# Hybrid decoder layer, one core: four units of the dilated projection as seven products, with the seventh product's bank copied out by VectorE

## The chip, the cores and the metric

The kernel runs on one core of a Trainium2 chip. The metric is the device time of one execution in microseconds, the median of several runs. A core has five engines that run their own instruction streams in order and wait for each other through semaphores: TensorE (PE) for matmuls, VectorE (DVE), ScalarE (ACT), GpSimd (POOL) and SyncE (SP), which here only issues transfers. Sixteen DMA engines move the data of all queues.

## The reference

One decoder layer on x of 256 x 2048 in float32:

```
h = rms_norm(x, g_attn); proj = h @ w_in          # 2048 x 10248
o_a = fox_attention(...)        # 8 heads of 128
o_b = dilated_attention(...)    # 8 heads of 128
merged = sigmoid(ga) * (o_a @ w_br_fox) + sigmoid(gb) * (o_b @ w_br_dil)   # each 1024 x 2048
x = x + merged @ w_out
h = rms_norm(x, g_ffn)
x = x + conv_ffn(h)             # 2048 -> 2 x 5632, causal convolution, SwiGLU, -> 2048
```

The change is in `o_b @ w_br_dil`: 256 rows, K = 1024 (eight heads of 128), 2048 columns.

## The kernel before

**Units.** The weights come in tiles of two K blocks by 512 columns (128 x 1024 numbers, 512 KB). A tile is a unit, and units have one running number. SP loads the tile (into one of four slots of `raw`, or into `raw_x` and `raw_y` for sums), ScalarE writes its high part into one of six slots of a ring (`w_hi`, function `high`, L1480), VectorE subtracts to get the low part (`w_lo`, `low`, L2086). TensorE then makes three matmuls of 512 columns for each K block and each half of the rows: 2 x 2 x 3 = 12 for a plain unit (`rows_unit`, L874 to L878). `high(n + RING)` stands behind unit n in ScalarE's program: it waits for the tile and for TensorE to have used unit n, and everything behind it in ScalarE's program waits with it. The load of a `raw` tile waits until the tile four loads earlier has been split (`lo_done`).

**Seven products.** The gates' projection, the output projection and the FFN already use a scheme of seven products in place of eight for a 2 x 2 arrangement of blocks (`("H", ...)` units, 6 matmuls each). Some products need sums of weight tiles. These are made by a transfer of the first tile and further ones that POOL issues with `accum_op=ALU.add` (L2814), which add into the tile in SBUF.

**The stage.** The last seven units before it are of the gates (`c` = 6). Then the Fox projection, 16 units: column blocks c = 0 to 3 of 512, and for each c four units u over K. Then the dilated projection, 16 units likewise, into the banks that `br_banks` gives. Then the output projection. The dilated heads 12 to 15 are worked in the Fox stage, head 12 + c beside column block c. TensorE's order is:

```
for u in range(4):
    branch_unit(c, u)
    if u == 0:
        if c:
            last_values(c - 1)
        attend_scores(q_of(3)[:, c, :], lambda a, b: k_of(3)[:, c, a:b])
    elif u == 3:
        attend_transpose(12 + c)
```

After the scores VectorE runs `softmax_head(12 + c, prep, True)` behind `low` of the unit six ahead. ScalarE makes the exponentials (`exps`) behind `high` of the same unit. After F(c,3) TensorE transposes the probabilities; ScalarE copies them out of the bank with `copy_pt(12 + c)` (L1492), behind `high` of F(c,3) + 6; and `last_values(c)` (L959, L960), behind the first unit of the next column block, waits for that copy. POOL prepares the bias of the heads 13 to 15 (`prepare_dil`, L2788 and L2790), each behind the row maximum of the head before. In the first two units ScalarE also applies the last two gate sigmoids (L1732). VectorE multiplies a finished column block with its gate (`fox_part`, `dil_part`) and adds both branches (`merged`, L2433).

SP loads the first four tiles of the output projection's pairs (`raw_x`, `raw_y` from `w_out`) behind the loads numbered 14, 17, 20 and 23 of the branch stage.

Of the kernel before, what the change touches and what calls it, by code (L numbers as in the profile page):

```python
# [6 lines left out]
P = 128  # L7
# [102 lines left out]
OUT_UNIT = BR_UNIT + 4 * UPR  # L110
# [22 lines left out]
FF_UNIT = OUT_UNIT + len(OUTS)  # L133
GATE_PARTS = ("P3", "P5", "P6")


def raw_use(n):

    if n < GATE_UNIT:
        return n % RAW_SLOTS, n // RAW_SLOTS + 1  # L140
    if n < BR_UNIT:
        k = GATE_LOAD_AT[GATES[n - GATE_UNIT]]
    elif n < OUT_UNIT:
        k = n - BR_UNIT + len(GATE_LOADS)
    else:
        k = OUT_LOAD_AT[OUTS[n - OUT_UNIT]] + 4 * UPR + len(GATE_LOADS)
    return k % RAW_SLOTS, (GATE_UNIT + k) // RAW_SLOTS + 1

# [41 lines left out]
def br_banks(m):  # L190
    return (0, 2) if m % 2 else (1, 3)
# [7 lines left out]
PAIR_LOADS_AT = {14: (1, 0), 17: (1, 1), 20: (0, 0), 23: (0, 1)}  # L199
# [9 lines left out]
TAIL_MADE = {"P5": 13, "P6": 14, "P7": 15, "P3": 16}  # L209
# [60 lines left out]
FIRST_SLOTS = (8, 9, 0, 1, 2, 3)  # L270
# [29 lines left out]
def load_count(k):  # L300

    before = raw_use(FF_UNIT - 1)[1] if slot_of(k) < RAW_SLOTS else 0
    return before + sum(slot_of(m) == slot_of(k) for m in range(k + 1))
# [34 lines left out]
def decoder_layer(nc, x, x_t, smalls, consts, w_in, w_fox, w_dil, w_out, w_up, w_down, decay_dram, out):  # L338
# [15 lines left out]
    with ctx:  # L354
# [116 lines left out]

        def last_of(name, k):
# [70 lines left out]
        def last_sum(m):  # L543
# [25 lines left out]
        xt_in = [sem(f"xt_in{u}") for u in range(UPR)]  # L569
        smalls_in, consts_in, wf_in, x_again, out_done = (  # L570
            sem("smalls_in"), sem("consts_in"), sem("wf_in"), sem("x_again"), sem("out_done"))
        second_tile, third_tile = sem("second_tile"), sem("third_tile")
        first_tile, gains_in, tile_high, tile_split, warm_data = (
            sem("first_tile"), sem("gains_in"), sem("tile_high"), sem("tile_split"), sem("warm_data"))
# [38 lines left out]
        d_seeded = sem("d_seeded")  # L613
        row_max, den_ready, rden_ready, dil_merged, tap1, ss_ready, fa_sum, fa_neg = (
            sem("row_max"), sem("den_ready"), sem("rden_ready"), sem("dil_merged"), sem("tap1"),
            sem("ss_ready"), sem("fa_sum"), sem("fa_neg"))
        decay_rows = [sem(f"decay_rows{m}") for m in range(4)]
# [8 lines left out]
        def _(sp):  # L626
# [11 lines left out]
            def load_late(n, src):  # L638

                if n >= BR_UNIT + RAW_SLOTS:  # L640
                    sp.wait_ge(lo_done, n - RAW_SLOTS)
                s = raw_use(n)[0]
                sp.dma_start(raw[:, s, :].rearrange("p (k n) -> p k n", k=KU), src).then_inc(w_loaded[s], 16)

            def br_tile(m):
                c, u = m // 4 % 4, m % 4
                return (w_fox_v if m < 16 else w_dil_v)[:, KU * u:KU * u + KU, NB * c:NB * c + NB]
# [91 lines left out]
            for n, unit in enumerate(GATES, GATE_UNIT):  # L739
                if unit[0] != "H":  # L740
# [4 lines left out]
                    else:  # L745
                        m = k - len(GATE_LOADS)
                        load_late(BR_UNIT + m, br_tile(m))
# [11 lines left out]
            for m in range(RAW_SLOTS, 4 * UPR):  # L759
                load_late(BR_UNIT + m, br_tile(m))  # L760
                if m in PAIR_LOADS_AT:
                    side, q = PAIR_LOADS_AT[m]
                    if side:
                        sp.wait_ge(lo_done, GATE_AT["H", PAIRS - 1, "P4", q])
                        load_gate_b22(PAIRS, q)
                    else:
                        sp.wait_ge(y_added[q], 2 * PAIRS)
# [96 lines left out]
        def _(pe):  # L864
# [273 lines left out]
            def branch_unit(m, u):  # L1138
                pair = [bank[b] for b in br_banks(m)]
                kt = KU * u if m < 4 else KT // 2 + KU * u  # L1140
                rows_unit(BR_UNIT + 4 * m + u, actB, (kt, kt + 1), pair, u == 0, u == 3)
# [23 lines left out]
            for c in range(4):  # L1165
                if c < 2:
                    pe.wait_ge(fox_merged, 3 + c)
                else:
                    pe.wait_ge(dil_merged, c - 1)
                for u in range(4):  # L1170
                    if c == 0 and u == 1:
                        pe.wait_ge(kept_lo, 1)
                    elif c == 0 and u > 1:
                        pe.wait_ge(o_lo, 12 + 2 * (u - 1))
                    branch_unit(4 + c, u)
                    if c == 0 and u == 0:
                        last_values(3)
                    if c and u == 2:
                        pe.wait_ge(merged, c)
                        transpose_block(lambda r, col: tmp[:, r, col:col + P], bank[4:6], mt_ready)  # L1180
# [7 lines left out]
            def out_product(n, name, q):  # L1188

                if q == 0:  # L1190
                    if name == "P3":
                        pe.wait_ge(dil_merged, 3)
                        pe.wait_ge(h_part_lo, 5)
                    elif name == "P1":
                        pe.wait_ge(dil_merged, 4)
                        pe.wait_ge(h_part_hi, 9)
                    elif name == "P7":
                        pe.wait_ge(h_part_lo, 6)
                    elif name == "P6":
                        pe.wait_ge(h_part_lo, 7)  # L1200
                        pe.wait_ge(g_p1, PAIRS + 1)
                    elif name == "P5":
                        pe.wait_ge(h_part_lo, 8)
# [36 lines left out]
            for n, unit in enumerate(OUTS, OUT_UNIT):  # L1240
# [6 lines left out]
                else:  # L1247
                    u = unit[1]
                    if u == 0:
                        pe.wait_ge(g_c22, PAIRS)  # L1250
# [98 lines left out]
            def tail_product(n, name):  # L1349
# [11 lines left out]
                if name in TAIL_PARTS:  # L1361
                    pe.wait_ge(h_part_lo, 8 + TAIL_PARTS.index(name) + 1)
# [60 lines left out]
        def _(act):  # L1423
            def high(n):
# [3 lines left out]
                if pair_product(n):  # L1428
# [14 lines left out]
                    else:  # L1443
                        act.wait_ge(y_added[q], 2 * c + 2)
                elif n < FF_UNIT:
# [328 lines left out]

            for c in range(4):
                for u in range(4):
                    high(BR_UNIT + 4 * c + u + RING)
# [7 lines left out]
                    elif u == 3:  # L1785
                        copy_pt(12 + c)

            for c in range(4):
                for u in range(4):
                    high(BR_UNIT + 16 + 4 * c + u + RING)  # L1790
                    if c == 0 and u == 0:
                        out_high(15)
                    elif c and u == 2:
                        merged_high(c - 1)
                    elif c == 3 and u == 1:
                        act.wait_ge(mt_lo, 2)
                        merged_part_high("P3", 12)
                        for half in range(2):
                            nc.scalar.activation(own[:, 0, :, half * P:half * P + P],
                                                 gate_quarter(0, 0, half).bitcast(f32), ACT.Copy, scale=-1.0)\  # L1800
# [1140 lines left out]
```

## Time and profile before

| | |
|---|---|
| median of 3 runs | 1331.04 us (1330.64 to 1331.25) |
| the profiled execution: its time | 1331.1 us |
| its span, first to last instruction | 1329.3 us |
| TensorE busy | 1324.8 us of it |
| VectorE, ScalarE, GpSimd busy | 1147.9, 959.9, 167.1 us |
| moved by the DMA engines | 312.03 MB, mean 235 GB/s |
| the Fox stage, first to last matmul | 456.2 to about 506 us |
| the dilated stage | about 506 to 545 us |

Times in the profile count from the start of the span. Each matmul of 512 columns is recorded with 0.39 us but starts 0.227 us after the one before, since they overlap. The DMA share is the mean busy share of the core's 16 DMA engines.

### The profile page before, as it was taken

The page shows a single profiled execution, that of the slowest core. Times are in us where ns is not written, and L with a number is a line of the kernel's source. Part 1 is how long each engine was busy: PE and PEld are TensorE (multiplying, and loading weights), DVE is VectorE, ACT ScalarE, POOL GpSimd, SP SyncE. Part 2 cuts the span into 40 slices and gives each one's busy share as a digit, 9 for nine tenths or more (in the row PEclk, how much of TensorE's full clock was granted, in tenths as well). Part 3 has the DMA queues.
Part 4 walks back from the last instruction along what each step waited for, and adds up shares of the span by engine and source line. Part 5 has one row for each costly group of instructions (what it writes and reads, how often), then busy time and mean ns, then how long its engine had stood idle before and what let it go on. Part 6 is the DMA issues. An engine that isn't in the chain of part 4 may idle for free.

```text
span 1329.3 us, 16539 instructions
## 1 busy us (share of the span) xinstructions
PE 1324.8 (100%) x6037; PEld 1098.8 (83%) x6037; DVE 1147.9 (86%) x1369; ACT 959.9 (72%) x1214; POOL 167.1 (13%) x186
## 2 busy tenths in 40 slices
PE   9999999999999999999999999999999999999999
PEld 7888888888888888888888888888888888888887
DVE  6868887888878876888689898999999999999998
ACT  6666666566666654567777878888888888888874
POOL 0121212021011000101010101111111102020201
DMA  9877685758888665488879798999989899999996
GB/s 355 290 170 262 142 259 119 244 156 229 230 218 226 219 207 205 129 238 260 288 174 332 161 303 172 314 220 282 248 252 267 230 281 222 294 213 315 192 294 176
DMA packets 120720, 312.03 MB, mean 235 GB/s; under 512 B 12088, under 2 KB 13376, under 8 KB 120384
## 3 DMA queue, kind: packets, MB, share of 16 engines
q1 hardware_dynamic: 92192, 235.10, 50.9%
q0 software_dynamic: 23824, 71.84, 30.4%
q10 hardware_dynamic: 4624, 4.05, 1.0%
q8 instruction: 48, 0.79, 0.2%
q14 instruction: 32, 0.26, 0.1%
HBM read 308.84 MB, written 2.11 MB: 234 GB/s over the span
## 4 chain that ended last, share of the span: by engine, by line
PE 100%; DVE 0%; POOL 0%; issue 0%; POOLq 0%
PE acc L874 12%; PE acc L878 12%; PE acc L876 12%; PE acc L912 9%; PE acc L916 9%; PE acc L914 9%; PE acc L1103 4%; PE acc L1099 4%; PE acc L1101 4%; PE acc L1076 3%; PE acc L1078 3%; PE acc L1074 3%; PE acc L1266 1%; PE acc L897 1%; PE acc L893 1%; PE acc L895 1%
## 5 line engine op out<-in xcount | busy, mean ns | idle before, releaser
L2086 DVE TENSOR_TENSOR w_lo<-raw,w_hi 128x1024 fp32r<-128x1024 f32 x225 | 272.7, 1219 | 67.1 <-ACT w_hi L1480 65.7
L1480 ACT ACTIVATE w_hi<-raw 128x1024 fp32r<-128x1024 f32 x225 | 235.1, 1054 | 86.7 <-PE acc L878 50.2
L874 PE MATMUL acc<-w_hi,actA 128*128 128x512 f32 x580 | 228.3, 394 | 0.0
L878 PE MATMUL acc<-w_hi,actA 128*128 128x512 f32 x580 | 226.1, 390 | 0.0
L876 PE MATMUL acc<-w_lo,actA 128*128 128x512 f32 x580 | 225.8, 389 | 0.0
L1480 ACT ACTIVATE w_hi<-raw_y 128x1024 fp32r<-128x1024 f32 x152 | 158.1, 1058 | 72.9 <-PE acc L878 21.9
L2086 DVE TENSOR_TENSOR w_lo<-raw_y,w_hi 128x1024 fp32r<-128x1024 f32 x152 | 182.8, 1219 | 18.4 <-ACT w_hi L1480 16.8
L2086 DVE TENSOR_TENSOR w_lo<-raw_x,w_hi 128x1024 fp32r<-128x1024 f32 x116 | 139.8, 1220 | 45.4 <-ACT w_hi L1480 45.2
L1480 ACT ACTIVATE w_hi<-raw_x 128x1024 fp32r<-128x1024 f32 x116 | 119.8, 1052 | 47.9 <-DMA raw_x<-w_in 23.0
L878 PEld LDWEIGHTS acc<-w_hi,actA 128*128 128x128 f32 x580 | 108.9, 188 | 22.9
L874 PEld LDWEIGHTS acc<-w_hi,actA 128*128 128x128 f32 x580 | 108.9, 188 | 21.9 <-issue 0.2
L876 PEld LDWEIGHTS acc<-w_lo,actA 128*128 128x128 f32 x580 | 109.0, 188 | 21.8
L912 PE MATMUL acc<-w_hi,actB 128*128 128x512 f32 x296 | 116.3, 393 | 0.0
L916 PE MATMUL acc<-w_hi,actB 128*128 128x512 f32 x296 | 115.4, 390 | 0.0
L914 PE MATMUL acc<-w_lo,actB 128*128 128x512 f32 x296 | 115.1, 389 | 0.0
L1099 PE MATMUL acc<-w_hi,actA 128*128 128x512 f32 x224 | 88.3, 394 | 0.0
L1103 PE MATMUL acc<-w_hi,actA 128*128 128x512 f32 x224 | 87.3, 390 | 0.0
L1101 PE MATMUL acc<-w_lo,actA 128*128 128x512 f32 x224 | 87.2, 389 | 0.0
L1480 ACT ACTIVATE w_hi<-odd 128x1024 fp32r<-128x1024 f32 x64 | 67.5, 1054 | 19.6 <-PE acc L916 9.9
L2086 DVE TENSOR_TENSOR w_lo<-odd,w_hi 128x1024 fp32r<-128x1024 f32 x64 | 77.9, 1217 | 1.8 <-ACT w_hi L1480 1.8
L2857 POOL DMA_DIRECT2D raw_y<-w_up x34 | 29.5, 867 | 376.2 <-DVE w_lo L2086 376.0
L2561 DVE SCALAR_TENSOR_TENSOR work<-acc,smalls_sb,work 128x255 f32<-128x255 f32 (+1 forms) x176 | 72.4, 472 | 3.2 <-ACT work L1863 3.1
(385 smaller groups left out, 2779.5 us busy)
## 6 DMA issues: line engine op xcount, KB each, us to landing
raw<-w_in SPq DMA_DIRECT2D x101, 512.0 KB, 4.8
raw<-w_down SPq DMA_DIRECT2D x59, 512.0 KB, 5.6
raw_x<-w_up SPq DMA_DIRECT2D x44, 512.0 KB, 5.0
raw_y<-w_up POOLq DMA_DIRECT2D x34, 512.0 KB, 7.6
raw_x<-w_in SPq DMA_DIRECT2D x28, 512.0 KB, 4.2
odd<-w_up SPq DMA_DIRECT2D x27, 512.0 KB, 5.1
work<-w_up SPq DMA_DIRECT2D x24, 512.0 KB, 5.5
work<-w_up POOLq DMA_DIRECT2D x24, 512.0 KB, 8.1
```

What stands on the lines that cost most here:

```text
L874: nc.tensor.matmul(o, lhsT=a_h, rhs=w_hi[:, s, k, :], start=first and k == 0, stop=False, skip_group_check=onto_seed)
L876: nc.tensor.matmul(o, lhsT=a_h, rhs=w_lo[:, s, k, :], start=False, stop=False, skip_group_check=onto_seed)
L878: mm = nc.tensor.matmul(o, lhsT=a_l, rhs=w_hi[:, s, k, :], start=False, stop=last and k == KU - 1, skip_group_check=onto_seed)
L912: nc.tensor.matmul(o, lhsT=a_h, rhs=w_hi[:, s, k, :], start=first and k == 0, stop=False, skip_group_check=True)
L914: nc.tensor.matmul(o, lhsT=a_h, rhs=w_lo[:, s, k, :], start=False, stop=False, skip_group_check=True)
L916: mm = nc.tensor.matmul(o, lhsT=a_l, rhs=w_hi[:, s, k, :], start=False, stop=last and k == KU - 1, skip_group_check=True)
L1099: nc.tensor.matmul(o, lhsT=a_h, rhs=w_hi[:, s, k, :], start=side == 0 and j == 0 and k == 0, stop=False, skip_group_check=True)
L1101: nc.tensor.matmul(o, lhsT=a_h, rhs=w_lo[:, s, k, :], start=False, stop=False, skip_group_check=True)
L1103: mm = nc.tensor.matmul(o, lhsT=a_l, rhs=w_hi[:, s, k, :], start=False, stop=kt == KT - 1, skip_group_check=True)
L1480: nc.scalar.activation(w_hi[:, n % RING, :, :], src.rearrange("p (k n) -> p k n", k=KU), ACT.Copy).then_inc(hi_done, 1)
L2086: nc.vector.tensor_tensor(w_lo[:, n % RING, :, :], src.rearrange("p (k n) -> p k n", k=KU), w_hi[:, n % RING, :, :].bitcast(f32), ALU.subt ...
L2561: t = nc.vector.scalar_tensor_tensor(out=conv[:, j, lag:SEQ], in0=bank[(4, 7)[j // 2]][:, (j % 2) * SEQ:(j % 2 + 1) * SEQ - lag], scalar=s ...
```

## The change

- Of the dilated projection the first two column blocks (c = 0, 1) with the first two K pairs (u = 0, 1), both row halves, are computed as seven products of 6 matmuls, in the order P1, P7, P6, P2, P5, P4, P3. The four other units of these column blocks follow as before (L(0,2), L(0,3), L(1,2), L(1,3)) onto the same banks, and the column blocks 2 and 3 are unchanged but for their banks.
- P1, P2 and P3 read a weight tile as it is. P4, P6, P7 and P5 read sums of 4, 3, 2 and 2 tiles. Their first tiles are loaded by SP behind the branch loads 4 to 7 (the tiles of F(1,0) to F(1,3)), the seven others added by POOL between its preparations of the heads 13, 14 and 15. They use `raw_x` and `raw_y`; the output projection's four pair tiles are loaded later (behind loads 22, 23, 24 and 26).
- The sums of the head outputs that five products need are made in the Fox stage: eight adds and four subtractions on VectorE, five high parts in six instructions on ScalarE.
- Between products ScalarE copies a bank three times (behind P1, P6 and P5). P7's bank is copied out by VectorE into the softmax tile, behind `out_low(15)`, the low part of the last head's output. `dil_gate(0)` and `dil_gate(1)` each have one more add, and `merge(1)` moves behind the first unit of column block 2.
- Some semaphores are shared and renumbered, and the slot order of the FFN's first tiles turns by one.

```diff
+DIL_STEPS = ("P1", "P7", "P6", "P2", "P5", "P4", "P3")
+DIL_BANKS = {"P1": 1, "P6": 1, "P5": 1, "P7": 7, "P4": 7, "P2": 3, "P3": 0}
+DIL_TILE = {"P1": (0, 0), "P2": (0, 1), "P3": (1, 1)}
+DIL_SUMS = {"P4": (0, ((1, 1), (1, 0), (0, 0), (0, 1))), "P6": (1, ((1, 1), (1, 0), (0, 0))),
+            "P7": (2, ((1, 1), (1, 0))), "P5": (3, ((0, 0), (1, 0)))}
+    units = [("F", c, u) for c in range(4) for u in range(4)]
+    units += [("Q", name) for name in DIL_STEPS] + [("L", c, u) for c in range(2) for u in (2, 3)]
+    return units + [("L", c, u) for c in (2, 3) for u in range(4)]
...
-PAIR_LOADS_AT = {14: (1, 0), 17: (1, 1), 20: (0, 0), 23: (0, 1)}
+PAIR_LOADS_AT = {22: (1, 0), 23: (1, 1), 24: (0, 0), 26: (0, 1)}
+DIL_BASE_AT = {4: "P4", 5: "P6", 6: "P7", 7: "P5"}
...
+            for m in range(RAW_SLOTS, len(BR_LOADS)):
+                load_branch(m)
+                if m in DIL_BASE_AT:
+                    load_dil_base(DIL_BASE_AT[m])
...
+            def dil_product(name):
+
+                if name == "P1":
+                    pe.wait_ge(fox_merged, 3)
+                    pe.wait_ge(h_part_hi, 8)
+                elif name == "P7":
+                    pe.wait_ge(g_c22, PAIRS)
+                elif name == "P6":
+                    pe.wait_ge(dil_out, DIL_OUT["P1"])
+                elif name == "P2":
+                    pe.wait_ge(kept_lo, 1)
+                elif name == "P5":
+                    pe.wait_ge(dil_out, DIL_OUT["P6"])
+                elif name == "P4":
+                    pe.wait_ge(dil_rows, 1)
+                elif name == "P3":
+                    pe.wait_ge(dil_out, DIL_OUT["P5"])
...
+            def dil_copy(n, name):
+
+                act.wait_ge(used, n + 1)
+                if name == "P1":
+                    act.wait_ge(fox_merged, 3)
+                    nc.scalar.activation(bank[3], bank[1], ACT.Copy, scale=-1.0).then_inc(dil_out, 1)
+                elif name == "P6":
+                    nc.scalar.activation(dil_v, bank[1], ACT.Copy, scale=-1.0).then_inc(dil_out, 1)
+                else:
+                    act.wait_ge(fox_merged, 4)
+                    nc.scalar.activation(bank[0], bank[1], ACT.Copy).then_inc(dil_out, 1)
...
+                low(BR_AT[unit] + RING)
+                if unit == ("Q", "P7"):
+                    out_low(15)
+                    dve.wait_ge(used, BR_AT[unit] + 1)
+                    nc.vector.tensor_copy(dil_p7, bank[7]).then_inc(dil_rows, 1)
...
-            for c in range(1, 4):
-                prepare_dil(12 + c).then_inc(prep_ready, 1)
+            def add_dil_tile(name, m):
+
+                at, tiles = DIL_SUMS[name]
+                c, u = tiles[m]
+                if m == 1:
+                    pool.wait_ge(dil_loaded[name], 32)
+                else:
+                    pool.wait_ge(dil_summed[name], 16 * (m - 1))
+                nc.gpsimd.dma_start(dil_at[at].rearrange("p (k n) -> p k n", k=KU),
+                                    w_dil_v[:, KU * u:KU * u + KU, NB * c:NB * c + NB], accum_op=ALU.add)\
+                    .then_inc(dil_summed[name], 16)
+
+            add_dil_tile("P4", 1)
+            add_dil_tile("P6", 1)
+            prepare_dil(13).then_inc(prep_ready, 1)
+            add_dil_tile("P7", 1)
+            add_dil_tile("P5", 1)
+            add_dil_tile("P4", 2)
+            prepare_dil(14).then_inc(prep_ready, 1)
+            add_dil_tile("P6", 2)
+            add_dil_tile("P4", 3)
+            prepare_dil(15).then_inc(prep_ready, 1)
```

## Rows read from the trace of the kernel before

**Rows 1.** The page: busy time of the engines, and the chain that ended last.

```profile
PE 1324.8 (100%) x6037; PEld 1098.8 (83%) x6037; DVE 1147.9 (86%) x1369; ACT 959.9 (72%) x1214; POOL 167.1 (13%) x186
...
PE 100%; DVE 0%; POOL 0%; issue 0%; POOLq 0%
```

**Rows 2.** TensorE's waits over the span: engine line, for whom, us, times, longest.

```profile
PE acc L999 <- POOL actB L2802: 1.3, 1, 1.3
```

**Rows 3.** TensorE in order of time: start us, length us, what.

```profile
1.31 4.21 PE L999 MATMUL acc<-actB 128*128 128x512 f32 x9 [1.31 <-POOL actB L2802]
...
7.59 0.40 PE L970 MATMUL acc<-w_hi,actA 128*128 128x512 f32 x1
...
456.25 0.39 PE L874 MATMUL acc<-w_hi,actB 128*128 128x512 f32 x1
...
458.74 0.39 PE L878 MATMUL acc<-w_hi,actB 128*128 128x512 f32 x1
...
467.81 0.49 PE L952 MATMUL acc<-smalls_sb,softmax 128*128 128x128 f32 x3
...
470.89 0.59 PE L959 MATMUL acc<-softmax,odd 128*128 128x256 f32 x2
```

**Rows 4.** ScalarE in order of time, 456 to 471 us.

```profile
456.44 0.60 ACT L1723 ACTIVATE work<-acc 128x512 f32<-128x512 f32 x1 [0.66 <-PE acc L1103]
...
469.19 1.04 ACT L1480 ACTIVATE w_hi<-raw 128x1024 fp32r<-128x1024 f32 x1
470.14 0.47 ACT L1492 ACTIVATE softmax<-acc 128x384 f32<-128x384 f32 x1
```

**Rows 5.** Stretches: busy time (instructions) of each engine, granted clock, DMA share, GB/s.

```profile
383.00:389.00 6.00, 6.00 (x28) 4.95 (x27) 5.28 (x5) 4.28 (x5) 1.20 (x1) 1.00 0.96 150
404.00:412.00 8.00, 8.00 (x37) 6.64 (x36) 5.72 (x7) 3.95 (x5) 1.07 (x1) 1.00 0.89 334
449.00:457.00 8.00, 8.00 (x37) 6.64 (x36) 5.87 (x7) 4.14 (x6) 0.00 (x0) 1.00 0.84 288
457.00:470.00 13.00, 13.00 (x62) 10.78 (x61) 8.12 (x18) 10.41 (x14) 1.00 (x2) 1.00 0.58 201
470.00:490.00 20.00, 20.00 (x95) 16.72 (x94) 15.60 (x35) 10.93 (x20) 2.02 (x4) 1.00 0.69 235
490.00:505.00 15.00, 15.00 (x72) 12.46 (x71) 11.03 (x21) 6.83 (x11) 0.00 (x0) 1.00 0.55 178
```

**Rows 6.** Single transfers issued at 443.2, 425.0, 413.1, 452.8: count, size, us to landing.

```profile
raw<-w_fox SPq DMA_DIRECT2D x1, 512.0 KB, 3.6
...
raw_x<-w_in POOLq DMA_DIRECT2D x1, 512.0 KB, 5.9
...
raw<-w_in SPq DMA_DIRECT2D x1, 512.0 KB, 8.0
...
raw<-w_fox SPq DMA_DIRECT2D x1, 512.0 KB, 4.5
```

**Rows 7.** VectorE in order of time, 460 to 472 us.

```profile
460.32 1.23 DVE L2086 TENSOR_TENSOR w_lo<-raw,w_hi 128x1024 fp32r<-128x1024 f32 x1 [0.47 <-ACT w_hi L1480]
...
464.80 0.55 DVE L2125 TENSOR_SCALAR softmax<-softmax,st 128x128 f32<-128x128 f32 x2
...
470.46 1.28 DVE L2422 TENSOR_TENSOR work<-acc,work 128x512 f32<-128x512 f32 x2
...
473.93 0.42 DVE L2130 TENSOR_TENSOR actB<-acc,actB 128x256 fp32r<-128x256 f32 x1
```

**Rows 8.** SP's issues of the tiles of F(1,0), F(1,3) and F(2,1).

```profile
449.43 0.37 SPq L643 DMA_DIRECT2D raw<-w_fox  x1
...
455.74 0.37 SPq L643 DMA_DIRECT2D raw<-w_fox  x1
...
459.28 0.37 SPq L643 DMA_DIRECT2D raw<-w_fox  x1
```

**Rows 9.** GpSimd, the preparation of head 14.

```profile
475.52 0.18 POOL L2788 COPY st<-smalls_sb 128x1 f32<-128x1 f32 x1 [11.71 <-DVE st L2105]
```

More of the change, by code:

```diff
@@ L133 @@
 FF_UNIT = OUT_UNIT + len(OUTS)
+OUT_AT_LOADS = [OUT_AT[unit] for unit in OUT_LOADS]
 GATE_PARTS = ("P3", "P5", "P6")
@@ L1163, in _, with turn_merged @@
                         attend_transpose(12 + c)
[L1165 to L1180 removed]
+            def turn_merged(c):
+                pe.wait_ge(merged, c + 1)
+                transpose_block(lambda r, col: tmp[:, r, col:col + P], bank[4:6], mt_ready)
+            for unit in BRANCH[16:]:
+                if unit[0] == "Q":
+                    dil_product(unit[1])
+                    if unit[1] == "P7":
+                        last_values(3)
+                    continue
+                _, c, u = unit
+                if c < 2:
+                    pe.wait_ge(o_lo, 12 + 2 * (u - 1))
+                    rows_unit(BR_AT[unit], actB, (KT // 2 + KU * u, KT // 2 + KU * u + 1),
+                              (bank[0], bank[1]) if c else (bank[3], bank[7]), False, u == 3, True)
+                    if c and u == 3:
+                        turn_merged(0)
+                    continue
+                if u == 0:
+                    pe.wait_ge(dil_merged, c - 1)
+                branch_unit(4 + c, u)
+                if u == 2:
+                    turn_merged(c - 1)
             def turn_x2(c):
@@ L2423, in fox_part, with dil_gate, merge @@
                 t.then_inc(fox_merged, 1)
-            def dil_part(c):
-                dve.wait_ge(used, BR_UNIT + 16 + 4 * c + 4)
-                for r in range(RT):
-                    part = gb[:, r, c * NB:(c + 1) * NB]
-                    t = nc.vector.tensor_tensor(part, bank[br_banks(4 + c)[r]], part, ALU.mult)
-                t.then_inc(dil_merged, 1)
+            def dil_gate(c):
+                dve.wait_ge(used, BR_AT["L", c, 3] + 1)
+                rows = [gb[:, r, c * NB:(c + 1) * NB] for r in range(RT)]
+                first, second = [bank[b] for b in ((3, 7), (0, 1), br_banks(6), br_banks(7))[c]]
+                if c == 0:
+                    dve.wait_ge(dil_out, DIL_OUT["P6"])
+                    nc.vector.tensor_tensor(dil_v, second, dil_v, ALU.add).then_inc(dil_rows, 1)
+                    second = dil_v
+                elif c == 1:
+                    dve.wait_ge(dil_rows, 1)
+                    nc.vector.tensor_tensor(dil_p7, second, dil_p7, ALU.subtract).then_inc(dil_rows, 1)
+                    second = dil_p7
+                nc.vector.tensor_tensor(rows[0], first, rows[0], ALU.mult)
+                if c < 2:
+                    dve.wait_ge(dil_rows, c + 2)
+                nc.vector.tensor_tensor(rows[1], second, rows[1], ALU.mult).then_inc(dil_merged, 1)
+            def merge(c):
                 dve.wait_ge(dil_merged, c + 1)
```

271 lines of the change are left out of this document (198 added, 73 removed).

## The prediction

> **What bounds the kernel now.** I read the page first. TensorE is busy for the whole span and the chain that ended last is TensorE throughout [rows 1]; the list of TensorE's waits has a single entry, at the very start [rows 2]. So nothing starves the matmuls, and an edit can only help by taking matmuls away, and can hurt as soon as it makes TensorE wait once. Next I read TensorE's instructions in order around the change. Inside a unit the matmuls of 512 columns start 0.227 us apart (456.25 to 458.74 for the first and the twelfth) and the next unit follows at once [rows 3]. The same timeline shows what hangs between units: at 467.81 the transposes of head 12, and at 470.89 its values product, whose first weight load starts 0.23 us before it. The reader should then look at ScalarE: the copy that this product waits for, `copy_pt(12)`, runs from 470.14 to 470.61, at once behind two splits [rows 4]. That copy ends when TensorE is ready for it, with no slack that I can see; it is only not listed as a wait because it just makes it. Last I read the DMA share by stage and the time of single transfers [rows 5, 6], because the change adds transfers.
>
> **What it removes.** The first two column blocks of the dilated projection, with the first two K pairs, are four units of 12 matmuls (48). Seven products of 6 take their place (42). Six matmuls at 0.227 us are 1.36 us off TensorE [rows 3]. The other units stay, 12 matmuls each.
>
> **What it adds on TensorE, ScalarE and VectorE in the product stretch.** Seven weight splits where there were four. A split is 1.04 us on ScalarE and 1.23 on VectorE [rows 4, 7], a product is 1.36 us, so each engine alone keeps up, with little over: in the 9.5 us of the products VectorE has seven splits (8.6), `out_low(15)` (0.42) and the new copy of bank 7, which I price as the bank read beside it (`fox_part`, 1.28 for two [rows 7]) at 0.64: 9.7. ScalarE has seven splits (7.3), three bank copies at 0.60 [rows 4] and `out_high`. The ring holds six split units, filled before the products begin (the splits for P1 to P3 are made while the units of 2.72 us run). The four hand-overs (P1's bank before P6, P6's before P5, bank 7 before P4, P5's before P3) each have one product of 1.36 us, or four products for bank 7, to cover a copy of about 0.6 plus 0.3 for the signal. Laid out in order, ScalarE's and VectorE's copies end 0.1 to 0.4 us ahead of their need; I take 0 and keep 2 as the upper end. Behind L(0,3), `dil_gate(0)` and `merge(0)` take 3 x 0.64 + 1.23 = 3.2 us, the 1.23 by an operation of the same 1024 columns [rows 7], and must be over when L(1,3) ends, 5.4 us later; they are queued behind a split whose tile now shares the queue with the four moved pair tiles. I take 0.6 us.
>
> The head sums (8 small adds on VectorE, four parts on each of ScalarE and VectorE, some 0.35 us each) lie in the Fox stage, where both engines are idle a third of the time; alone they cost 0. What covers them is that idle time; without it they would add their 4 to 5 us to the softmax chain below.
>
> **What it adds in transfers, the part that decides.** The four summed weights need 4 plain tiles and 7 accumulating ones; 3 more plain tiles replace 4. A plain tile of 0.524 MB takes 0.524/(334/0.89) = 1.40 us of all 16 DMA engines, an accumulating one 0.524/(150/0.96) = 3.36 us [rows 5]. Alone, they land 3.6 and 5.9 us after their issue [rows 6], so 2.2 and 2.5 us pass before their data flows. The extra is 4 x 1.40 + 7 x 3.36 = 29 us of DMA time. From 449 to 505 the engines now carry 0.84 x 8 + 0.58 x 13 + 0.69 x 20 + 0.55 x 15 = 36 of 56 us [rows 5]; three pair tiles (4.2) leave that stretch. 36 + 29 - 4 = 61: more than it holds. In the mean that could still be borne, since TensorE has six split units ahead; but the order matters.
>
> The four base tiles go onto SP's queue right behind F(1,0), F(1,1), F(1,2) and F(1,3), issued from 449.4 to 455.7 [rows 8]. None of SP's new waits holds it up (their splits come before that of F(0,0)). Queued behind them are F(2,0) and F(2,1), the second of them issued at 459.3 [rows 8]. POOL starts the first sums of P4 and P6 when their bases are there, about 456 and 458; P7's and P5's follow `prepare_dil(13)`, about 467. Now count what must flow before F(2,1)'s tile is there. Before, the tile of F(1,2) landed at 452.8 + 4.5 = 457.3. After that come F(1,3), F(2,0), F(2,1) and the four bases: 7 x 1.40 = 9.8, less 1.3 us in which the engines were free before (16% of 449 to 457) = 8.5. The two first sums add 6.7. That gives 457.3 + 8.5 + 6.7 = 472.5. By then the sum of P7 flows too (issue 467, data from 469.5), and that of P5 behind it. An accumulation beside a plain tile slows it more than by halves: the plain tile issued at 413.1 behind two of them landed 8.0 us later instead of 3.6 [rows 6], 1.40 us of work in about 5.8. With P7's whole sum ahead, F(2,1) lands at 475.9; with P5's too, at 479. I take 476 to 477.
>
> ScalarE runs in order: the split of F(2,1) is in front of `copy_pt(12)`. Landing 476.5, split 1.04, copy 0.47: 478.0. TensorE wants it at 470.9 less 0.2. The wait is about 7 us, once, between F(1,0) and F(1,1). Its bounds are 3.5 (472.5 + 1.5 - 470.7, no third sum in the way) and 10 (479). Head 12's softmax itself is late as well (F(1,2), whose split is in front of it, lands about 461.5, not 457.3), but its end was at 465.4 for a need at 467.8 [rows 3, 7], so that delay of 2 to 3 us is nearly covered. After the wait the DMA engines have gained 7 us, and the waits for heads 13 to 15 should be below 0.5 in all. Of POOL's queue: `prepare_dil(14)` stands behind two sums, `prepare_dil(15)` behind two more; the first had 11.7 us of idle time before it [rows 9], and the two sums that come in front take 3 to 4 us of POOL once their data is there.
>
> At this place a rule of the Trainium skill bears, "DMA: Bandwidth & Descriptors", section "SWDGE vs HWDGE vs iDMA": transfers of GpSimd and of SP feed different queues inside each DMA engine, which takes from them by turns. Turns at equal packets would give a plain tile 1.40/(1.40 + 3.36) = 29% of the time while a sum flows; 1.40 in 5.8 us is 24%, so the trace agrees roughly, and the wait would be 7 to 9 us by the rule.
>
> **The sum.** -1.4 (matmuls) + 6.5 (the wait for the copy of head 12, with its bounds 3.5 and 10) + 0.6 (merge) = +5.7 us. Against the profiled execution's own time, 1331.1 (span 1329.3 and 1.8 around it), that is 1336.8; its time stands 0.06 above the median of the runs, so 1336.7.
>
> **The rivals.**
> (A) The crowding is absorbed, so that it ends on the other side: not slower. The mechanism is one: SP's tiles keep their place, and F(2,1) lands before 469.2, when its split began before [rows 4]. For it: the six units ahead, and a landing of 4.5 us in a stretch with a share of 0.84 [rows 6, 5]. Against it: even with no sum in the way, 457.3 + 8.5 = 465.8 leaves 3.4 us, the length of one sum, and two flow. It decides at 3.4 us of sum time ahead of that tile. Time: 1331.1 - 1.4 + 0.0 to 0.6 = 1329.7 to 1330.3, no change.
> (B) Only the first sums are in the way, the wait is 3.5 or a little under: 1331.1 - 1.4 + 3.5 = 1333.2, or a bit less; at the border of what can be told.
> (C) The queue stays full: the waits come again at heads 13 and 14, because each head has two or three sums, or the pause slows what follows. At the start of the kernel nine matmuls after a pause took 4.21 us, and from 1.31 to 7.59 some fifteen took 6.3 us where 3.4 is the pace later [rows 3], so a pause can cost 2.9 us more. Time: 10 + 2.9 - 1.4 + 0.6 = 12, that is 1343. "TensorE: Matmul & The Clock Gate" in the Trainium skill, section "What's actually happening", says that the clock halves after an idle stretch; whether 7 us is such a stretch, no row of this trace shows.
> (D) The transfers are hidden, but the products starve on VectorE: 9.7 us of work in 9.5, and each late hand-over is a wait. +2 instead of 0: 1331.1 - 1.4 + 2 + 0.6 = 1332.3, within what can't be told.
>
> **How the numbers follow.** A measurement of this kernel can tell 0.2%, 2.7 us. Forecast 0.50, (A) 0.18, (B) 0.12, (C) 0.14, (D) 0.06. Slower are the forecast, (C) and a third of (B): 0.68. The same are (A), (D) and two thirds of (B): 0.32, of which I give 0.02 to faster, for which no mechanism is to be seen beyond 1.4 us. The time is that of the forecast, 1336.7. Its own range is 1333.5 to 1340 (wait of 3.5 to 10). For 8 in 10 it reaches down into (A), to 1330.0, and up into (C), to 1342.
>
> **What would show it.** Right: in the list of TensorE's waits one new line, a values product waiting for ScalarE's softmax copy (`copy_pt`), several us long, near 471; ScalarE's split before it waiting for the transfer of a Fox tile; landings of Fox tiles from 450 to 480 of 7 us and more, and a DMA share above 0.9 there. 42 matmuls in the products. Wrong: no wait of TensorE before 500, Fox landings still below 5.5 us, or a wait inside the seven products for a bank copy, which would make (D) the cause.

## The result, and the profile after

The changed kernel takes 1341.88 us, the median of 5 runs (1340.28 to 1344.05). In the same comparison the kernel before takes 1331.04 (1330.64 to 1331.43). The ratio is 1.0082, with a 95% interval of 1.0067 to 1.0097: 10.8 us slower. The forecast was 1336.7 in a range of 1330.0 to 1342.0. The direction held. The size was five us too small, mainly by two terms of the sum: the time lies outside the forecast's own range (1333.5 to 1340), nearer to the 1343 of rival (C) than to the forecast, and only 0.1 us inside the upper end of the wide range. The profiled execution took 1344.05 us, the slowest of the five, with a span of 1342.3. Of the experiments below, the version without the base tiles and the one with the pair tiles late each had one execution at a much lower granted clock (0.65 and 0.85; 1907.91 and 1473.36 us), and the median given for these two is that of the others.

The page of the changed kernel, busy time and the chain that ended last, against [rows 1]:

```profile
PE 1327.4 (99%) x6031; PEld 1099.5 (82%) x6031; DVE 1156.9 (86%) x1387; ACT 967.0 (72%) x1226; POOL 175.8 (13%) x193
...
PE 93%; DMA 4%; DVE 2%; ACT 1%; issue 0%; POOL 0%; ACTq 0%; POOLq 0%
```

TensorE has six matmuls fewer and yet 2.6 us more busy time: some of its matmuls ran slower. And for 7% of the span it is no longer what sets the end. The list of its waits, against the single entry of [rows 2], says where (columns: engine and line, for whom, us in total, times, longest):

```profile
PE acc L1024 <- ACT softmax L1608: 6.7, 1, 6.7
PE acc L990 <- DVE tmp L2601: 2.0, 1, 2.0
PE acc L1344 <- ACT odd L1964: 1.4, 1, 1.4
PE acc L1064 <- POOL actB L3017: 1.3, 1, 1.3
```

The first new line is the predicted one: the values product of head 12, waiting for `copy_pt(12)`. TensorE in order of time there, against [rows 3]:

```profile
470.60 0.39 PE L943 MATMUL acc<-w_hi,actB 128*128 128x512 f32 x1
477.68 1.22 PE L1024 MATMUL acc<-softmax,odd 128*128 128x256 f32 x2 [6.69 <-ACT softmax L1608]
...
480.05 0.98 PE L939 MATMUL acc<-w_hi,actB 128*128 128x512 f32 x1
480.83 0.44 PE L941 MATMUL acc<-w_lo,actB 128*128 128x512 f32 x1
481.11 0.40 PE L943 MATMUL acc<-w_hi,actB 128*128 128x512 f32 x1
```

Up to 470.6 both kernels run together; then nothing for 6.7 us. The reader should look at what follows as well: after the pause the values product and the scores of the next head take 2.37 us (477.68 to 480.05) for work that took 1.12 before, and only at 480.83 does the pace return to 0.23 us between starts.

What ScalarE did meanwhile, against [rows 4]:

```profile
468.58 1.06 ACT L1596 ACTIVATE w_hi<-raw 128x1024 fp32r<-128x1024 f32 x1 [2.40 <-DMA raw<-w_fox]
...
474.22 1.06 ACT L1596 ACTIVATE w_hi<-raw 128x1024 fp32r<-128x1024 f32 x1 [1.08 <-DMA raw<-w_fox]
476.19 1.06 ACT L1596 ACTIVATE w_hi<-raw 128x1024 fp32r<-128x1024 f32 x1 [0.91 <-DMA raw<-w_fox]
477.15 0.47 ACT L1608 ACTIVATE softmax<-acc 128x384 f32<-128x384 f32 x1
```

These are the splits of F(1,3), F(2,0) and F(2,1), each released by the landing of its tile, and behind the last one the copy, which ends at 477.62. The chain that ended last goes the same way (start, length, what); its first row is F(2,1)'s tile, 15 us from issue to landing:

```profile
461.12 15.05 DMA raw<-w_fox
...
477.15 0.48 ACT softmax L1608
477.68 1.22 PE acc L1024 x2
```

The stretches of [rows 5] in the changed kernel (busy time and instructions of TensorE, its weight loads, VectorE, ScalarE and GpSimd, then granted clock, DMA share, GB/s), with a short one at 539:

```profile
449.00:457.00 8.00, 8.00 (x37) 6.64 (x36) 5.20 (x6) 3.87 (x5) 0.36 (x1) 1.00 0.91 293
457.00:470.00 13.00, 12.97 (x61) 10.50 (x60) 7.03 (x17) 5.79 (x9) 4.20 (x5) 1.00 1.08 309
470.00:490.00 20.00, 13.31 (x56) 10.79 (x55) 12.62 (x26) 12.65 (x18) 5.83 (x6) 0.83 1.02 260
490.00:505.00 15.00, 15.00 (x72) 12.48 (x71) 13.03 (x26) 7.67 (x17) 1.00 (x2) 1.00 0.82 245
539.00:542.00 3.00, 3.00 (x8) 2.31 (x7) 3.00 (x5) 1.57 (x4) 0.00 (x0) 0.50 0.65 200
```

From 457 to 490 the DMA engines are full (1.08 and 1.02, where [rows 5] have 0.58 and 0.69). The granted clock, 1.00 in every stretch of [rows 5], is 0.83 in the mean of the stretch with the pause and 0.50 in the short one behind the second wait: there it is 1.2 GHz instead of 2.4 throughout.

The second wait is that of the first transposes of the merged rows for `merge(0)`, on VectorE. TensorE in order of time:

```profile
535.25 0.39 PE L943 MATMUL acc<-w_hi,actB 128*128 128x512 f32 x1
537.62 1.09 PE L990 MATMUL acc<-smalls_sb,tmp 128*128 128x128 f32 x8 [1.98 <-DVE tmp L2601]
```

VectorE in order of time:

```profile
533.28 1.23 DVE L2240 TENSOR_TENSOR w_lo<-raw,w_hi 128x1024 fp32r<-128x1024 f32 x1 [1.50 <-ACT w_hi L1596]
534.42 0.68 DVE L2586 TENSOR_TENSOR softmax<-acc,softmax 128x512 f32<-128x512 f32 x1
...
536.34 1.23 DVE L2601 TENSOR_TENSOR tmp<-work 128x1024 f32<-128x1024 f32 x1
```

VectorE stood for 1.50 us in front of the low part of L(2,2), because its tile landed late (532.2), and only then began the gate and merge.

Set against the kernel before by the starts of the same TensorE instructions, the loss builds up so:

| where | us |
|---|---|
| the wait for the copy of head 12 | +6.8 |
| the slow pace behind it, up to F(1,1)'s second matmul | +1.6 |
| the seven products, 42 matmuls for 48 | -1.36 |
| the wait for `merge(0)` | +2.0 |
| the slow pace behind it | +1.8 |
| sum | +10.84 |
| a third wait, at 594.79 (1.5 by starts), and 0.6 in small pieces | +2.1 |

(The first wait is entered by starts, 477.68 against 470.89 [rows 3]; the pace behind it by 480.83 less 477.68, 3.15 us, against 1.54 before.) The last row takes the sum to the profiled execution's own 1344. 1331.04 + 10.84 = 1341.9 is also the median. That is no proof of the single rows for the other executions: by the medians of the experiments below the first wait with its pace is 8.7 us and the second 2.5.

### The profile page after: what moved, and what is told of

Read it like the earlier page. It is cut to its first block, busy times and chain, and to the rows that moved or that the text cites. A ratio compares the mean times of both kernels' runs of the same rounds, so it can differ in the third digit from the quotient of the medians.

```text
span 1342.3 us, 16579 instructions
## 1 busy us (share of the span) xinstructions
PE 1327.4 (99%) x6031; PEld 1099.5 (82%) x6031; DVE 1156.9 (86%) x1387; ACT 967.0 (72%) x1226; POOL 175.8 (13%) x193
## 4 chain that ended last, share of the span: by engine, by line
PE 93%; DMA 4%; DVE 2%; ACT 1%; issue 0%; POOL 0%; ACTq 0%; POOLq 0%
PE acc L939 11%; PE acc L943 11%; PE acc L941 11%; PE acc L977 9%; PE acc L981 9%; PE acc L979 9%; PE acc L1164 3%; PE acc L1168 3%; PE acc L1166 3%; PE acc L1139 3%; PE acc L1141 3%; PE acc L1143 3%; DMA raw<-w_fox 2%; DVE w_lo L2240 1%; PE acc L1378 1%; PE acc L958 1%
```

## The experiments

The theory is that of the prediction: the transfers crowd out the tile of F(2,1), ScalarE's split stands in front of `copy_pt(12)`, and TensorE waits. To it the profile added that each pause also costs slow matmuls. The rivals are that the four base tiles alone do it, that the four moved pair tiles matter, and that it is the amount of transfers, not their place.

**The sums left out** (and then the base tiles too).

```
-            add_dil_tile("P4", 1)
-            add_dil_tile("P6", 1)
             prepare_dil(13).then_inc(prep_ready, 1)
-            add_dil_tile("P7", 1)
...
-                    act.wait_ge(dil_summed[summed_product(n)], 16 * (len(tiles) - 1))
+                    act.wait_ge(dil_loaded[summed_product(n)], 32)
```

> The changed kernel without its seven accumulating transfers; the four base tiles are still loaded, and the splits of P4, P6, P7 and P5 read them as they are (four products use unsummed weights). Crowding theory: without 7 x 3.36 us of DMA time F(2,1) lands near 466, before 469.2, so TensorE's 6.7 us wait for head 12's copy and the slow pace behind it (1.5) go; the wait of 2.0 before the first transposes of the merged rows, with 1.9 of slow pace, stays, because the pair tiles are where they were: 1331.0 - 1.4 + 3.9 = about 1333.6. Rival, the new work on ScalarE and VectorE (parts, sums, copies) holds up the head's chain: the 6.7 us wait stays and the time is 1340 or more.

Measured: 1335.87 us (1334.15 to 1338.29), ratio 1.0036 (1.0023 to 1.0049). TensorE's waits, then the stretch with the pause:

```profile
PE acc L990 <- DVE tmp L2601: 2.1, 1, 2.1
PE acc L1024 <- ACT softmax L1608: 1.5, 1, 1.5
```

```profile
470.00:490.00 20.00, 18.49 (x88) 15.16 (x87) 17.56 (x35) 11.29 (x19) 1.01 (x2) 1.00 0.50 170
```

The first wait falls from 6.7 to 1.5 us, with no slow matmul behind it (clock 1.00). So the sums are 5.2 us of this wait, and its slow pace on top: the theory's main part is shown. The rest comes another way than expected. The tile of F(2,1) lands at 467.7, in time. But F(1,2)'s lands at 460.99, and in the kernel before its split began at 459.23. Head 12's exponentials, the gate's sigmoid and the splits of F(2,0) and F(2,1) follow that split on ScalarE without a tile to wait for, so the copy is late from there. The time is 2.3 us above the expected 1333.6, and this wait is 1.5 of it. The rival, the new work on ScalarE and VectorE, falls. The second wait stays.

> As the one without sums, and the four base tiles are not loaded either, so the four summed products split what lies in raw_x and raw_y (unrelated weights). Crowding theory with sums as the whole cause of the first wait: the same time as without the sums alone, about 1333.6, since plain tiles fit. If the base tiles alone were enough to delay the Fox tiles, this one is faster than the other by up to the difference of their first waits (0 to 3 us).

Measured: 1332.69 us, the median of nine (1331.55 to 1335.06), ratio 1.0013 (1.0004 to 1.0023; its profiled execution 1331.57). The wait for the copy is gone; one remains:

```profile
PE acc L988 <- DVE tmp L2598: 1.8, 1, 1.8
```

The base tiles are the remaining 1.5 us of the first wait. The second wait does not depend on any of the eleven added transfers. It is shorter by 0.3 us than without the sums alone, and no slow matmul follows it.

**The pair tiles late.**

```
-PAIR_LOADS_AT = {22: (1, 0), 23: (1, 1), 24: (0, 0), 26: (0, 1)}
+PAIR_LOADS_AT = {26: (1, 0), 27: (1, 1), 28: (0, 0), 30: (0, 1)}
```

> The changed kernel with the four pair tiles of the output projection issued behind the loads 26, 27, 28 and 30 in place of 22, 23, 24 and 26. Theory for the second wait: L(2,2)'s tile is late because the pair tiles share SP's queue with it; its split holds dil_gate(0) and merge(0) back. Then the wait of 2.0 us before the first transposes goes, and the slow pace behind it, 1341.9 - 3.9 = about 1338.0. Rival, VectorE's own work behind the seven products is what makes merge(0) late: the wait stays and the time is 1341.9.

Measured: 1339.3 us, the median of three (1338.97 to 1339.98), ratio 1.0062 (1.0042 to 1.0082).

```profile
PE acc L1024 <- ACT softmax L1608: 6.5, 1, 6.5
...
PE acc L1139 <- ACT work L1829: 0.5, 1, 0.5
```

The second wait is gone and so is its slow pace (clock 1.00 from 530 to 545); the first stands. So the four moved pair tiles, in front of L(2,2)'s tile on SP's queue, make the second wait. The gain is about 2.6 us, against the 3.8 that the table gives to the wait and its pace and the 3.9 expected: by the intervals of the two ratios both are possible. The wait of 0.5 in the list has nothing to do with it: it stands at 100.0 us, long before this stage.

**The rows behind the merge.** VectorE does the low part of L(2,2) behind the gate and merge instead of ahead of them.

```
+                if unit == ("L", 0, 2):
+                    continue
+                if unit == ("L", 0, 3):
+                    low(BR_AT["L", 0, 2] + RING)
```

> The changed kernel with its transfers as they are, but on VectorE the low part of L(2,2)'s tile stands behind dil_gate(0) and merge(0) instead of in front of them. Theory for the second wait (the merge is queued behind a split whose tile is late): merge(0) ends 3.3 us after L(0,3), before L(1,3) ends, and the wait of 2.0 goes as it did with the pair tiles late, about 1339.6. Rival (the pair tiles' effect came through something else): the wait stays, 1341.9.

Measured: 1340.09 us, ratio 1.0068 (1.0054 to 1.0082). The list of waits, then TensorE at the transposes for `merge(0)` and at those for `merge(1)`:

```profile
PE acc L990 <- DVE tmp L2601: 0.9, 1, 0.9
```

```profile
536.07 0.39 PE L943 MATMUL acc<-w_hi,actB 128*128 128x512 f32 x1
536.29 1.04 PE L990 MATMUL acc<-smalls_sb,tmp 128*128 128x128 f32 x8
...
546.39 1.09 PE L990 MATMUL acc<-smalls_sb,tmp 128*128 128x128 f32 x8 [0.87 <-DVE tmp L2601]
```

The wait for `merge(0)` is gone, as expected: its transposes start 0.22 us after the matmul before them, and the clock stays at 1.00 from 530 to 545. The 0.9 in the list is a new wait for `merge(1)`, up to which VectorE works without a pause from 538.6 on. So the second wait needs both, a late tile and the low part of that tile in front of the merge: take away either and it is gone. The gain is 1.8 us in the medians.

**TensorE kept busy in the pause.** 28 matmuls of 512 columns into bank 7, which nobody uses then, ahead of head 12's values product.

```
+                        if c == 1:
+                            pe.wait_ge(g_c22, PAIRS)
+                            for _ in range(28):
+                                nc.tensor.matmul(bank[7][:, :], lhsT=actB[:, 8, 0:P], rhs=actB[:, 8, :], start=True,
+                                                 stop=True)
```

> The changed kernel with 28 matmuls of 512 columns into the unused bank 7 in the place where TensorE waits for head 12's copy (28 x 0.227 = 6.3 us of a 6.7 us wait). Theory that idleness lowers TensorE's clock and that this costs 1.5 us behind the wait: granted clock 1.00 in 470 to 490, first matmul of F(1,1) about 1.5 us earlier, 1341.9 - 1.5 = 1340.4. Rival, the slow stretch comes from the transfers in flight and not from the pause: the steps of 0.43 us behind the wait stay and the time is 1341.9.

Measured: 1339.51 us (1338.35 to 1341.5), ratio 1.0063 (1.0048 to 1.0078). TensorE in order of time, and the stretch:

```profile
471.45 6.51 PE L1267 MATMUL acc<-actB 128*128 128x512 f32 x28
...
479.50 0.58 PE L939 MATMUL acc<-w_hi,actB 128*128 128x512 f32 x1
```

```profile
470.00:490.00 20.00, 19.69 (x91) 16.09 (x90) 12.32 (x24) 13.49 (x20) 5.83 (x6) 1.00 1.02 265
```

The clock stays at 1.00 (0.83 in the changed kernel). From the last matmul of F(1,0) to the second of F(1,1) it is 8.69 us instead of 10.23: the copy is as late as ever, and 1.54 us come back. This tells the slow pace apart from the wait; it is a cost of its own, about 1.5 us. The rival, that the transfers in flight slow the matmuls, falls, since they are as they were (DMA share 1.02). The medians gave 2.4 us back (1341.88 less 1339.51), and the ranges of the two overlap.

**The copy ahead of the split.** ScalarE does `copy_pt` before the weight split with which it shares the step.

```
+                    if u == 3:
+                        copy_pt(12 + c)
                     high(BR_AT["F", c, u] + RING)
...
-                    elif u == 3:
-                        copy_pt(12 + c)
```

> The changed kernel with ScalarE's copy_pt(12 + c) ahead of the split of F(c,3) + 6 instead of behind it, for all c. Theory (the wait is a copy queued behind a split whose tile is late): head 12's copy is then held only by the split of F(2,0), whose tile landed at 474.2, so it ends near 475.7 instead of 477.6; the first wait is 4.8 instead of 6.7 us and the time 1341.9 - 1.9 = about 1340. Rival (the copy waits for the transposes or for VectorE's softmax): no change.

Measured: 1339.56 us (1338.38 to 1341.01), ratio 1.0066 (1.005 to 1.0081). ScalarE, then TensorE's waits:

```profile
473.71 0.47 ACT L1608 ACTIVATE softmax<-acc 128x384 f32<-128x384 f32 x1
```

```profile
PE acc L1024 <- ACT softmax L1608: 3.8, 1, 3.8
```

The copy no longer stands behind the split of F(2,1), and comes 3.4 us earlier than in the changed kernel. Of these, 1.5 are the split of F(2,0) in front of it, which began at 472.75 instead of 474.22, and 1.9 are the order on ScalarE. A wait of 3.8 remains, because the tile of F(2,0) is late as well. The time gained less than the wait, 2.3 for 2.9: the slow pace lasted longer here, with starts 0.43 us apart up to about 480, and cost 2.9 us instead of 1.6 (by starts, as in the table); the clock of 470 to 490 is again 0.83. A shorter pause was no cheaper in slow matmuls.

**Half of each sum.** Each accumulating transfer brings only its first K block, 256 KB.

```
-                nc.gpsimd.dma_start(dil_at[at].rearrange("p (k n) -> p k n", k=KU),
-                                    w_dil_v[:, KU * u:KU * u + KU, NB * c:NB * c + NB], accum_op=ALU.add)\
+                nc.gpsimd.dma_start(dil_at[at].rearrange("p (k n) -> p k n", k=KU)[:, 0:1, :],
+                                    w_dil_v[:, KU * u:KU * u + 1, NB * c:NB * c + NB], accum_op=ALU.add)\
```

> The changed kernel in which each accumulating transfer adds only the first of the tile's two K blocks (256 KB), so that the second half of the four summed weights lacks its summands. Crowding theory: three half sums ahead of F(2,1) are 5.0 us instead of 10.1, its tile lands near 472 and the copy ends at 473.5: a first wait of 2.5 to 3 us, between the 1.5 without sums and the 6.7 of the full ones, and a time of 1337 to 1338. Rival (the number of transfers or POOL's descriptor work counts, not their bytes): the wait stays above 5 us.

Measured: 1334.31 us (1333.7 to 1337.87), ratio 1.0032 (1.0022 to 1.0043). A miss:

```profile
PE acc L990 <- DVE tmp L2601: 1.8, 1, 1.8
PE acc L1024 <- ACT softmax L1608: 1.4, 1, 1.4
```

I expected a wait of 2.5 to 3, in the middle. It is as short as with no sums. The tile of F(2,1) now lands at 469.6, so that the copy is set by the late F(1,2) again, as without sums. The cost of the sums is not in proportion to their bytes: in these runs the wait is longer only where F(2,1) is the later of the two. (The median is 1.5 us below that without sums, within the two intervals; in the profiled executions no slow matmul follows the second wait here, where the clock was 0.56 from 532 to 535 without sums.)

**The same transfers, spread.** All eleven stay. The bases are issued behind F(1,2), F(2,0), F(2,2) and F(3,1), P7's first, instead of behind F(1,0) to F(1,3); GpSimd's sums go between the preparations in the order in which the products need them; the pair tiles as in the late version.

```
-DIL_BASE_AT = {4: "P4", 5: "P6", 6: "P7", 7: "P5"}
+DIL_BASE_AT = {6: "P7", 8: "P4", 10: "P6", 13: "P5"}
...
-            add_dil_tile("P4", 1)
-            add_dil_tile("P6", 1)
             prepare_dil(13).then_inc(prep_ready, 1)
             add_dil_tile("P7", 1)
-            add_dil_tile("P5", 1)
-            add_dil_tile("P4", 2)
+            add_dil_tile("P4", 1)
             prepare_dil(14).then_inc(prep_ready, 1)
+            add_dil_tile("P6", 1)
+            add_dil_tile("P4", 2)
             add_dil_tile("P6", 2)
-            add_dil_tile("P4", 3)
             prepare_dil(15).then_inc(prep_ready, 1)
+            add_dil_tile("P4", 3)
+            add_dil_tile("P5", 1)
```

> The changed kernel with the same eleven transfers spread over the stage, and the pair tiles late as in the earlier experiment: bases of P7, P4, P6, P5 behind the loads 6, 8, 10 and 13, and POOL's order prepare 13, P7+1, P4+1, prepare 14, P6+1, P4+2, P6+2, prepare 15, P4+3, P5+1. Crowding theory: up to 460 nothing but P7's base lies in front of the Fox tiles, F(2,1) lands before 466, no wait at head 12; the sums end before 507, in time for P4 and P5. The wait list holds no entry above 1 us, and the time is 1331.0 - 1.4 + 0 to 2 = 1329.7 to 1331.7. Rival (the amount of transfers decides and not their place, 61 us of work in 56): the waits move to heads 14 and 15 or to the products, and the time is 1335 or more.

Measured: 1330.69 us (1330.21 to 1332.46) beside 1331.25 for the kernel before, ratio 0.9998 (0.9989 to 1.0006). The wait and the stretches:

```profile
PE acc L1024 <- ACT softmax L1608: 0.2, 1, 0.2
```

```profile
457.00:470.00 13.00, 13.00 (x61) 10.81 (x60) 8.46 (x18) 9.93 (x14) 3.39 (x4) 1.00 1.01 307
470.00:490.00 20.00, 19.82 (x93) 16.24 (x92) 17.91 (x36) 10.87 (x20) 5.35 (x7) 1.00 1.07 286
490.00:505.00 15.00, 15.00 (x72) 12.46 (x71) 12.55 (x30) 9.20 (x18) 2.62 (x3) 1.00 0.91 236
```

The DMA share is as high as in the changed kernel, and TensorE does not wait. The tile of F(2,1) lands at 466.3, and the Fox tiles issued from 450 to 465 take 6.5 us in the median, not 14.1; GpSimd issues its first sum at 464.4 instead of 456.6. So the rival "it is the amount" falls: it is which tile stands in front of which. The whole loss is given back, 11 us; what is left of the 1.4 us gain is too small to tell.

Two versions of it tell the second wait apart. With the pair tiles early again:

> The paced kernel with the four pair tiles where the change had put them (behind loads 22, 23, 24 and 26). It prices the second wait by itself: no wait at head 12, one of about 2 us before the first transposes of the merged rows, and behind it 0 to 1.9 us of slow pace, 1330.7 + 2 to 3.9 = 1332.7 to 1334.6. Rival (the second wait came from the first, which shifted VectorE's and the transfers' order): no wait, 1330.7.

Measured: 1333.19 us (1331.92 to 1334.38), ratio 1.0014 (1.0005 to 1.0023). TensorE, and the stretch around it:

```profile
529.31 1.09 PE L990 MATMUL acc<-smalls_sb,tmp 128*128 128x128 f32 x8 [2.25 <-DVE tmp L2601]
...
530.86 0.63 PE L943 MATMUL acc<-w_hi,actB 128*128 128x512 f32 x1
```

```profile
530.00:545.00 15.00, 15.00 (x66) 12.38 (x65) 12.64 (x16) 8.38 (x13) 0.00 (x0) 0.89 0.57 190
```

The second wait is back with its slow pace, alone and without the first: the moved pair tiles are its cause, and not the state in which the first wait left the queues. It costs 2.5 us (1333.19 less 1330.69). This version differs from the changed kernel in nothing but the place of the eleven transfers, and is 8.7 us faster (1341.88 less 1333.19): the first wait and its slow pace, 8.4 in the table.

With the spread transfers, the late pair tiles, the copy ahead of the split and the merge ahead of the low part:

> The paced kernel with both changes of order in addition: ScalarE's copy_pt ahead of the split, VectorE's merge(0) ahead of the low part of L(2,2). The paced kernel's span ended 0.6 us before that of the kernel before, of 1.36 us that six matmuls are worth, with one wait of 0.2 us left at head's copy. Theory (the rest is in the waits for in-order copies): 0.2 us more, 1330.5. Rival (the rest is in the starts of the products, whose operands change more often): the same time as paced, 1330.7. Either way within what a measurement can tell from the kernel before, and no wait above 0.2 in the list.

Measured: 1330.48 us (1329.78 to 1330.65) beside 1331.23, ratio 0.9993 (0.9984 to 1.0002), the fastest median of all, and still not to be told from the kernel before. Its one wait of 0.7 us, at 536.7, is again for `merge(1)`; I had expected none above 0.2.

## Why the prediction was right, and what it mis-sized

- **TensorE bounds, six matmuls less are 1.36 us.** Right: the 42 matmuls run without a wait inside, and the spread version, with one 0.2 us wait, comes out within 0.1% of the kernel before.
- **The hand-overs of the products, 0.** Right: none is in the list of waits, and rival (D) falls. The 0.3 us put down for a signal was too much where it can be read: head 12's copy ends at 477.62 and the matmul that waits for it starts at 477.68.
- **The wait for the copy of head 12, +6.5.** Right in place and cause: 6.7 in the list, 6.8 by starts. The size fits too, but the sum does not follow from the working: that gives 478.0 - 470.7 = 7.3, and the sum carries 6.5 without a reason (with 7.3 the forecast would have been 1337.5). Landing of F(2,1) at 476.2 for 476 to 477, end of the copy at 477.6 for 478.0. The theory was tested from both sides: without sums 1.5 us, with half of each 1.4, with the same transfers spread 0.2. One step under it was less right. The prediction called the delay of head 12's softmax, behind the late split of F(1,2), nearly covered. For the transposes that is so. But the late split of F(1,2) also moves the sigmoid, the splits of F(2,0) and F(2,1) and the copy behind them, which was not counted; where F(2,1) is in time, this is a wait of 1.4 to 1.5.
- **How fast a tile goes beside a sum.** 1.40 us of work in 5.8 us was taken from one tile of [rows 6]. In the changed kernel the first sum of P4 took 10.0 us from issue to landing (5.9 for such a transfer in [rows 6]). From the landing of F(1,2) at 461.5 to that of F(2,1) at 476.2 five plain tiles landed, with one to three sums under way: 7.0 us of work in 14.7, 48%, so plain tiles and sums shared the engines about evenly. The landing of F(2,1) came out right all the same; I take it that it hardly depends on the shares, since the engines were full and nearly all of both kinds was in front of it, but no run tests that. The rule of turns from "DMA: Bandwidth & Descriptors" in the Trainium skill, section "SWDGE vs HWDGE vs iDMA", would have left the sum 71% here; the trace does not bear that out, and the wait, 6.8, came out just under the 7 to 9 us of the rule.
- **The pause slows what follows.** This was put into rival (C) only, with 2.9 us taken from the start of the kernel, where it should have been a term of the sum: +1.6 behind the first wait, 1.54 given back by the dummy matmuls. This is the first mis-sized term (0 for 1.6). The rule of the Trainium skill, "TensorE: Matmul & The Clock Gate", section "What's actually happening", that the clock halves after an idle stretch, holds here at a pause of 6.7 us: granted clock 0.83 over the stretch, and 1.00 where TensorE was kept busy.
- **merge(0), +0.6.** The second mis-sized term: a wait of 2.0 and 1.8 of slow pace behind it, 3.8 in the profiled execution, 2.5 to 2.6 in the medians of the versions that differ in the place of the pair tiles alone. The mechanism was named (queued behind a split whose tile shares the queue with the moved pair tiles), but its delay was not counted: the split of L(2,2) had to wait for a landing at 532.2, and the gate and merge take 3.2 us more. With the pair tiles late it is gone, and with the merge ahead of that low part too.
- **The sum.** 1331.1 - 1.36 + 6.8 + 1.6 + 2.0 + 1.8 = 1341.9. Without the two terms of `merge(0)` it is 1338.1, and the version with the pair tiles late, which has that wait no more, took 1338.97 in its profiled execution, 0.5 of it the wait at 100.0. That the recorded range held the measured time is in part luck: its upper end was drawn from (C), with a wait of 10 us that did not come and 2.9 of slow pace behind it; what filled the gap was slow pace behind two waits and the second wait itself.
- **The waits of heads 13 to 15, under 0.5 in all.** Right: none is listed. So (C) in its first form, that the queue stays full for TensorE, falls; its second form, the slow pace, holds: 1.6 and 1.8 us of the five that were missing.
- **Rival (A).** Its deciding point, 3.4 us of sum time ahead of F(2,1), fits the halved sums: there, the tile landed at 469.6, about at the border of 469.2 that (A) set, and the wait was no longer made by it. (A)'s outcome, no loss, came only where the transfers were spread.
- **GpSimd.** Two sums took 2.45 us of it, not 3 to 4; no wait of TensorE came from there.

Open: the third wait (1.4 us at 594.79, for ScalarE's rows, behind a tile that took 7.1 us to land) is in the profiled execution, the slowest of five. Whether the other four have it, no trace shows; none of the ten profiled versions above does, and the sum without it meets the median. The 0.8 us between the spread version (1330.69) and 1331.25 - 1.36 are less than what a measurement can tell.

## What to carry to other kernels

When TensorE has no wait at all, look for the hand-over that ends just as it is needed, and count what stands in front of it on the engine that makes it: a split waiting for a tile there is the way by which a crowded DMA queue reaches TensorE. Added transfers are costed by which tile they come before, and not by their sum: eleven of them cost 8.7 us more in one order than in another, in which they cost nothing that can be told. To a pause of TensorE add the slow matmuls behind it, here 1.6 to 2.9 us where the granted clock fell and nothing where it stayed. And read in the timeline to which instruction a wait in the list belongs: one line of the kernel can stand for several hand-overs.

## What the hardware showed that was not expected

- Behind some pauses of about 2 us the half clock came: behind the waits for `merge(0)` of 1.98 us (changed kernel, 0.50 from 539 to 542), 2.07 (no sums, 0.56 from 532 to 535), 2.19 (TensorE kept busy in the first pause, 0.67 from 536 to 539) and 2.25 (spread, pairs early, 0.58 from 530 to 533). Behind those of 1.80 (no base tiles), 1.76 (halved sums) and 1.61 (copy ahead of the split) the clock stayed at 1.00, as behind the waits of 1.4 and 1.5 us for the copy. So the second wait is cheap in one version and dear in another, though it is the same wait. Each of these is one execution, and what decides between them no run shows.
- The slow stretch did not grow with the pause: 6.7 us of waiting cost 1.6 us, 3.8 us cost 2.9 (the copy ahead of the split), 2.0 us cost 1.8.
- The engines' DMA share stood at 1.01 to 1.08 for 33 us both in the version that lost 11 us and in the one that lost none. The share does not tell the two apart; the landing of the Fox tiles issued from 450 to 465 does (14.1 us against 6.5).
